# Reordering the first loads of a one-core decoder-layer kernel: weight block 2 ahead of swt and x's tiles, x's first row whole, parameters in ScalarE's queue

## The reference

```python
xn = rms_norm(h, norm1_w[l])
proj = xn @ w_in[l] + b_in[l]
u, v, q, k, vg, r, g_lr, gate_a, gate_b = jnp.split(proj, split_points, axis=-1)
ya = chunked_sgu(jax.nn.gelu(u), jax.nn.gelu(v), sgu_ln_w[l], sgu_ln_b[l], sgu_w[l], sgu_b[l])
gk = jax.nn.log_sigmoid((g_lr @ w_gk2[l] + b_gk[l]).astype(jnp.float32)) / GLA_GATE_NORMALIZER
yb = gla(q, k, vg, gk, r, gla_norm_w[l])
merged = jax.nn.sigmoid(gate_a) * (ya @ w_branch_a[l]) + jax.nn.sigmoid(gate_b) * (yb @ w_branch_b[l])
h = h + merged @ w_out[l]
xn2 = rms_norm(h, norm2_w[l])
h = h + (jax.nn.silu(xn2 @ w_ffn_gate[l]) * (xn2 @ w_ffn_up[l])) @ w_ffn_down[l]
return rms_norm(h, final_norm_w)
```

## Time and profile before

| | us |
|---|---|
| median of 3 executions | 819.62 |
| lowest, highest | 818.04, 819.68 |
| the profiled execution | 818.88 |
| its span (first to last instruction) | 817.2 |
| TensorE busy in the span | 808.4 |
| ScalarE, VectorE, GpSimd busy | 440.5, 535.7, 413.1 |

### The profile page before, as it was taken

How to read it: one execution, slowest core, us unless ns; L and a number is a source line. 1 busy time by engine, 2 the same in 40 slices (tenths; PEclk the granted TensorE clock), 3 DMA queues, 4 the chain that set the end, 5 groups by cost and what they waited for, 6 DMA issues and landing times.

```text
span 817.2 us, 13355 instructions
## 1 busy us (share of the span) xinstructions
PE 808.4 (99%) x5500; PEld 749.6 (92%) x5500; DVE 535.7 (66%) x561; ACT 440.5 (54%) x502; POOL 413.1 (51%) x146
## 2 busy tenths in 40 slices
PE   8999999999999999999999999999999999999997
PEld 7788888888888899999998899999999999999985
DVE  5277277374774957888974278766667777677736
ACT  4533446756656645867442585444554446665624
POOL 3545425424224533477955443544444445878880
PEclk9999999999999999999999999999999999999999
DMA  8973422221133253322234202422234445436022
GB/s 334 222 250 128 155 103 79 76 103 52 52 104 105 102 206 105 103 103 105 85 131 201 103 1 103 144 107 107 108 108 159 161 156 190 173 123 216 1 78 103
DMA packets 27709, 103.11 MB, mean 126 GB/s; under 512 B 2832, under 2 KB 4496, under 8 KB 23696
## 3 DMA queue, kind: packets, MB, share of 16 engines
q1 hardware_dynamic: 22720, 88.12, 30.2%
q10 hardware_dynamic: 4944, 14.36, 5.7%
HBM read 94.08 MB, written 8.39 MB: 125 GB/s over the span
## 4 chain that ended last, share of the span: by engine, by line
PE 98%; DMA 0%; issue 0%; ACT 0%; SPq 0%; DVE 0%; ACTq 0%
PE acc L2118 14%; PE acc L2120 14%; PE acc L2121 14%; PE acc L1901 7%; PE acc L1903 6%; PE acc L1902 6%; PE acc L1918 6%; PE acc L1919 6%; PE acc L1920 6%; PE acc L2317 3%; PE acc L2316 3%; PE acc L2314 3%; PE acc L1949 3%; PE acc L2032 1%; PE acc L2071 1%; PE acc L2076 1%
## 5 line engine op out<-in xcount | busy, mean ns | idle before, releaser
L469 POOL TENSOR_TENSOR w_lo<-raw,w_hi 128x2048 fp32r<-128x2048 f32 x26 | 122.2, 4700 | 164.6 <-ACT w_hi L664 164.6
L490 POOL TENSOR_TENSOR A_lo<-wp,A_hi 128x1024 fp32r<-128x1024 f32 x51 | 126.0, 2470 | 144.7 <-ACT A_hi L840 137.4
L855 ACT ACTIVATE S_hi<-acc 128x1024 fp32r<-128x1024 f32 x68 | 68.1, 1024 | 89.5 <-PE acc L2121 56.3
L2120 PE MATMUL acc<-xt_lo,A_hi 128*128 128x256 f32 x408 | 115.5, 283 | 0.0
L2121 PE MATMUL acc<-xt_hi,A_lo 128*128 128x256 f32 x408 | 115.5, 283 | 0.0
L2118 PE MATMUL acc<-xt_hi,A_hi 128*128 128x256 f32 x408 | 115.5, 283 | 0.0
L1451 DVE TENSOR_TENSOR S_lo<-acc,S_hi 128x1024 fp32r<-128x1024 f32 x68 | 81.8, 1221 | 18.6 <-ACT S_hi L855 18.5
L1901 PE MATMUL acc<-xt_hi,w_hi 128*128 128x512 f32 (+1 forms) x240 | 92.5, 385 | 0.0
L1903 PE MATMUL acc<-xt_hi,w_lo 128*128 128x512 f32 (+1 forms) x240 | 91.7, 382 | 0.0
L1902 PE MATMUL acc<-xt_lo,w_hi 128*128 128x512 f32 (+1 forms) x240 | 91.7, 382 | 0.0
L664 ACT ACTIVATE w_hi<-raw 128x2048 fp32r<-128x2048 f32 x26 | 49.6, 1910 | 68.7 <-PE acc L1920 55.1
(11 more groups left out here) (325 smaller groups left out, 2333.4 us busy)
## 6 DMA issues: line engine op xcount, KB each, us to landing
wp<-wstream SPq DMA_DIRECT2D x34, 1024.0 KB, 7.0
raw<-wstream SPq DMA_DIRECT2D x26, 1024.0 KB, 4.9
wd<-wstream SPq DMA_DIRECT2D x16, 512.0 KB, 6.1
down_sums<-act_sum ACTq DMA_DIRECT2D x8, 512.0 KB, 3.2
sum_raw<-down_sums SPq DMA_DIRECT2D x8, 512.0 KB, 3.3
turned_sums<-tx ACTq DMA_DIRECT2D x4, 512.0 KB, 3.9
raw_out<-wstream SPq DMA_DIRECT2D x2, 1024.0 KB, 5.8
raw_ffn<-wstream SPq DMA_DIRECT2D x2, 1024.0 KB, 8.6
```

Of the source, the lines that this page charges most:

```text
L469: pool.tensor_tensor(w_lo[s][:, :], raw[s][:, :], w_hi[s][:, :], ALU.subtract).then_inc(lo_ready, 1)
L490: pool.tensor_tensor(low_of(name, rows), weights_of(name, c, rows), high_of(name, rows), ALU.subtract).then_inc(plain_low, 1)
L855: a.activation(high_of(name, rows), src, ACT.Copy).then_inc(op_high, 1)
L2120: pe.matmul(dst, wh[:, g, k, :], x[1][:, k, :], start=False, stop=False, skip_group_check=True)
```

## The change

SyncE no longer loads `par`; ScalarE does, ahead of the two quarters. Row 0 of x is one transfer, the first of SyncE's queue, and one activation of 512 columns instead of two of 256; TensorE waits for it once. Block 2's load, with its waits, is issued ahead of `swt` and the two x tiles, and block 3's after them, both taken out of the loop; GpSimd splits block 2 before it masks `swt` and block 3 after. The warming products are nine instead of eight.

```diff
-WARM_UP = 8
+WARM_UP = 9
...
-            sp.dma_start(par[:, :], cols).then_inc(par_landed, 16)
-            sp.dma_start(xw[:, 0, 0:HT], x_t[:, 0, 0:HT]).then_inc(x00_landed, 16)
-            sp.dma_start(xw[:, 0, HT:SEQ], x_t[:, 0, HT:SEQ]).then_inc(x0_landed[0], 16)
+            sp.dma_start(xw[:, 0, :], x_t[:, 0, :]).then_inc(x0_landed[0], 16)
             sp.dma_start(xw[:, 1, :], x_t[:, 1, :]).then_inc(x0_landed[1], 16)
             sp.dma_start(raw[0][:, D:BLK], wstream[0][:, D:BLK]).then_inc(raw_landed[0], 16)
             sp.dma_start(xw[:, 2:4, :], x_t[:, 2:4, :]).then_inc(xt_landed[1], 16)
             sp.dma_start(raw[1][:, :], wstream[1]).then_inc(raw_landed[1], 16)
             for q in range(2, 4):
                 sp.dma_start(xw[:, 2 * q:2 * q + 2, :], x_t[:, 2 * q:2 * q + 2, :]).then_inc(xt_landed[q], 16)
+            sp.wait_ge(block0_low, 2)
+            sp.wait_ge(hi_ready, 1)
+            sp.wait_ge(lo_ready, 1)
+            sp.dma_start(raw[0][:, :], wstream[2]).then_inc(raw_landed[0], 16)
             sp.dma_start(swt[:, :, :], sgu_wt).then_inc(swt_landed, 16)
             for t in range(2):
                 sp.dma_start(xn_in[:, t, :], x[t * P:(t + 1) * P, :]).then_inc(x_landed[t], 16)
-            sp.wait_ge(block0_low, 2)
-
-            with sp.Fori(1, B_OUT // 2) as i:
+            sp.wait_ge(hi_ready, 2)
+            sp.wait_ge(lo_ready, 2)
+            sp.dma_start(raw[1][:, :], wstream[3]).then_inc(raw_landed[1], 16)
+
+            with sp.Fori(2, B_OUT // 2) as i:
...
             low(1, 1, 16)
+            low(2, 0, 32)
             pool.wait_ge(swt_landed, 16)
...
-            with pool.Fori(1, B_OUT // 2) as i:
+            low(3, 1, 32)
+            with pool.Fori(2, B_OUT // 2) as i:
...
         def _(a):
+            a.dma_start(par[:, :], cols).then_inc(par_landed, 16)
             for hf in range(2):
...
             a.wait_ge(par_landed, 16)
-            w0 = par[:, K_N1:K_N1 + 1]
-            a.wait_ge(x00_landed, 16)
-            a.activation(xw_hi[:, 0, 0:HT], xw[:, 0, 0:HT], ACT.Copy, scale=w0).then_inc(x00_high, 1)
             a.wait_ge(x0_landed[0], 16)
-            a.activation(xw_hi[:, 0, HT:SEQ], xw[:, 0, HT:SEQ], ACT.Copy, scale=w0).then_inc(xw_hi_ready, 1)
+            x_high(0)
...
-            pe.wait_ge(x00_high, 1)
+            pe.wait_ge(xw_hi_ready, 1)
...
-                        if c == 0 and k == 0 and lh is xw_hi and w is w_hi and hf == 0 and t == TT // 2:
-                            pe.wait_ge(xw_hi_ready, 1)
```

More of the change, by code:

```diff
@@ L262, in build @@
         x0_landed = [sem(f"x0_landed{k}") for k in range(2)]
-        x00_landed, x00_high = sem("x00_landed"), sem("x00_high")
         xw_hi_ready, xw_ready = sem("xw_hi_ready"), sem("xw_ready")
```

## The result

| | before | after |
|---|---|---|
| median of 20 runs | 819.30 us | 821.48 us |
| lowest, highest | 817.68, 821.23 | 819.94, 824.52 |
| profiled execution, its span | 818.88 (817.2) | 821.2 (819.5) |

The ratio is 1.0038, with an interval of 1.0030 to 1.0046: the change costs 3.1 us, and the forecast was 1.0 us to the good. The medians are only 2.2 us apart and the means 2.9: the ratios of this document weigh all executions, the long tail of after with them. Seven of the twenty runs of after are above 822 us; no run of before is. The same kernel measured once more (`e12_repeat`, at the end of the experiments) gave 1.0023, so 1.9 us (1.0013 to 1.0033); the two intervals overlap a little.

The account below looks back on a forecast made before the run. The prediction took the kernel to be bound by TensorE, a line of matmuls busy 99% of the span. Block 2's wait (-1.62) and the second quarter (+0.6) gave 819.62 - 1.0 = 818.6 us, range 817.4 to 820.0 for 8 in 10.

Parts of the forecast that it names:

- The bound, and where the end is set: TensorE busy 99% of the span; changes in the first 30 us move the end as they move block 2's first matmul.
- Block 2's transfer: Block 2's load ahead of swt and x's tiles: issued about 13.9, landed 19.0, low part ended 25.5.
- What it is worth: TensorE's wait at block 2 goes, first matmul at 27.90 instead of 29.45: 1.62 us gained, bounds nothing and 1.62.
- The second quarter: Block 0's second quarter, behind par and the first quarter, lands 7.1: 0.6 us lost, bounds gain 0.35 and loss 2.3.
- the slow rival: At the second quarter's cast: the quarter is as late as row 1 was, price 2.3 us, net 820.3; chance 0.10.
- The byte count over both queues: Landing of block 0's second quarter: 1.3 MB to move in both queues, giving 7.5, taken as 7.1.
- The clock: TensorE before its first real matmul: the 0.92 us gap had cost no clock, so the ninth pass gains none.
- VectorE locked behind GpSimd: Row 5's low part ends near 26.1 instead of 22.6; up to 1.5 us lost if block 2 is late; chance 0.05.
- The sum: Whole kernel: -1.62 + 0.6 = -1.0 us, taking 819.62 to 818.6 us.

Follow-up runs that it names:

- e12_repeat: The changed kernel measured once more, unchanged: median 820.58 us, ratio 1.0023 to the kernel before.
- e1: Kernel before with only block 2's load and split moved ahead of swt and x's tiles: median 819.72 us, ratio 1.0007.
- e5: e1 with ScalarE's three loads (x tiles 2 and 3, the bias) issued after the first tile's sum of squares: median 818.68 us, ratio 0.9995.
- e4: Kernel before with 4 warming passes instead of 8: median 819.75 us, ratio 1.0013.
- e11: Kernel before with 10 warming passes instead of 8, block 2 where it was: median 818.49 us, ratio 0.9995.
- e8: e5 with 10 warming passes instead of 8: median 817.53 us, ratio 0.9987 to the kernel before.
- e2: Kernel before with only the changed start (row 0 whole, parameters in ScalarE's queue, nine passes): median 820.20 us, ratio 1.0020.
- e9: The changed kernel with ScalarE's three loads issued after the first tile's sum of squares, nine passes: median 821.37 us, ratio 1.0033 to the kernel before.
- e10: e9 with 13 warming passes instead of 9: median 819.98 us, ratio 1.0021 to the kernel before.
- e7: Kernel before with only row 0 of x loaded and scaled whole, par still first in SyncE's queue: median 818.71 us, ratio 1.0001.
- e6: Kernel before with only par's load moved to the head of ScalarE's queue: median 818.66 us, ratio 1.0000.
- e3: The changed kernel with 13 warming passes instead of 9: median 819.67 us, ratio 1.0028 to the kernel before.

## Why the prediction was wrong

**The bound, and where the end is set: right.** Start of block 2 plus 787.6 to 787.8 us gives the span in 13 of the 14 profiles of this case; in e1 it is 788.1, for its wait at block 6.

**Block 2's transfer: right in mechanism, early in time.** Predicted: issued 13.9, landed 19.0, low part ended 25.5. Measured: 12.70, 17.4, 27.74. The issue was early because block 0's low parts were, its other half having been issued 0.9 us sooner: GpSimd's ended at 11.52 (before, 13.72). It did not follow that one, though, but VectorE's two halves, which ended at 12.67; the prediction had GpSimd's alone set the issue. The low part was late because its buffer's high part has to wait for TensorE, which I had not counted. The wait of 1.55 us went, as forecast.

**What it is worth: the first step that failed.** "1.55 + 0.07 = 1.62 us" holds only if TensorE arrives at 27.90 and block 2 is ready at 29.4, and I took both from one execution. In e1 and e5, whose start is before's own, TensorE came at 29.92 and 29.62; in e4 and e11, whose loads are before's own, the low part was done by 28.7. The wait was slack for a start that varies by up to 2 us; its removal alone is worth nothing measurable (e1, 1.0007; e5, with block 3 mended, 0.9995, both intervals around 1). With a steadier start the kernel is below before (e8: 817.53, 1.15 us at the median).

**The second quarter: the term that was mis-sized.** Predicted: landed 7.1, second four matmuls 7.63, loss 0.6. Measured: 8.17, 8.68, and 1.64. It landed 0.07 past the point from which the slow rival decides ("from a landing after 8.1 on"), to which I gave one in ten; in e2, e9, e10 and e12 it was about as late. The byte count over both queues had given 7.5, and I took 0.4 off it for the 1 KB rows that go; going that way was the error. The measured 8.17 lies midway between that byte count and row 1's 8.8 behind the same bytes. The first quarter was late too: predicted 5.3, bound 5.85, measured 5.88, and so the first matmul at 6.47 and not at 5.83.

**The clock: the step that failed outright.** "The granted clock is 1.00 in every stretch that I read, the one with the 0.92 us gap before 5.79 too, so the gap had cost no clock and the pass gains none." In the row that I read, 1.00 is also what stands ahead of the first rise, and so says nothing there. The level has to be read from the distance of equal matmuls: 0.427 us at the lower, 0.227 at the upper. For before's one execution the sentence comes out right, its clock having risen at 4.62, by luck: of the nine profiles of this case with eight or nine passes, five (e1, e5, e7, after, e12) had it rise only in the middle of the real matmuls. In after's it cost 2.18 of the 3.82 us. The sum had no term for it, no rival had it either, and for the runs above 822 us I found no other cause: e9's, at 821.91, is the nearest that was profiled. Those at 823 and 824 were not, and what they did stays open.

**VectorE locked behind GpSimd: right in kind, at another place.** The rival was for block 2's time. It happened at 9.2 us: the two low halves took 3.47 us beside GpSimd's 2.63, where before they had VectorE to themselves; 1.28 us for two in e6. With the matmuls at the lower level it was hidden; in e3, with them at the upper one, TensorE waited 0.5 us for it. I had those halves end at 9.8, and they ended at 12.67. The Trainium skill (SBUF — State Buffer, SBUF: two separate sides) has one of the two engines hold a shared port pair for its whole instruction and the other blocked; the 3.47 agrees, as the two halves end 1.15 us after GpSimd's instruction, near the 1.28 us that they take alone. These halves are also what block 2's issue waited for, 1.2 us longer than for GpSimd.

**The sum.** Predicted -1.62 + 0.6 = -1.0. Profiled: -1.55 + 1.64 + 2.18 = +2.3. Of the error of 3.3 us, 1.0 is the quarter and 2.2 the clock. With the size of the quarter right and the clock left out, I would have said 819.6, no change; the 821.48 of the median needs the clock.

## What to carry over

A wait near the end of a start-up is also a cushion: before it is priced at its full length, ask what spread of the work ahead of it it hides, and look at two or three executions, not at one, for both of its ends. Read TensorE's level from the distance between equal matmuls in the timeline, above all before the first rise, and keep TensorE at work without a gap up to and into the first real matmuls (in the four profiles with ten or thirteen passes the upper level was there by 6.8 us at the latest); passes that end half a microsecond early, or a transfer that is late by a microsecond, can cost more than themselves. As far as the landings of e2, e6 and e7 tell, when two queues share the engines, moving a small load out of one and merging two loads in it lets the rest of that queue go sooner, and what the other queue carries on the critical path pays.

## What was not expected of the hardware

- A gap of 1.42 to 1.71 us in TensorE's first real matmuls was followed by the lower clock level in three profiles (e2, e8, e9), for 3.4 to 6.8 us; gaps of 0.44 and 0.82 us (e6, e3) were not, nor was one of 1.35 us in e10. What decides it in a given execution stays open.
- After the same eight or nine passes the upper level was reached at very different times: the first real matmuls of before, e2, e6 and e9 were 0.23 to 0.34 us apart from the start, those of e1, e5 and e12 not until 9.7 to 9.8 us, those of e7 not until 12.6, those of after not until 13.1. After, e9 and e12 have one and the same start, and so have before, e1 and e5.
- The same transfer of 0.13 MB, row 0's second half, landed 4.1, 5.0 and 5.8 us after its issue in three executions with one and the same start (before, e1, e8).
- Two edits, each without effect (1.0000 and 1.0001), cost 0.20% together and with a ninth pass.
